# High and low rows of the activations as one 512-column product in the second layer's output and feed-forward projections

## The reference, cut to what matters

```python
def sq_relu_mlp(h, w1, w2):
    return jnp.square(jax.nn.relu(h @ w1)) @ w2
...
        xs = xs + g1 * ox
        xs = xs + g2 * sq_relu_mlp(rms_norm(xs, norm_mlp_g[l]) * (1 + sc2) + sh2, mlp_w1[l], mlp_w2[l])
```

## Time and profile before

| | us |
|---|---|
| median of 3 runs | 1467.81 |
| lowest and highest run | 1464.56, 1473.18 |
| profiled execution, its time | 1474.42 |
| profiled execution, its span | 1472.6 |
| TensorE busy in the span | 1405.8 (95%) |
| VectorE busy | 768.9 (52%) |
| ScalarE busy | 698.8 (47%) |

### The profile page before, as it was taken

How to read it: one execution, slowest core, us unless ns; L and a number is a source line. 1 busy time by engine, 2 the same in 40 slices (tenths; PEclk the granted TensorE clock), 3 DMA queues, 4 the chain that set the end, 5 groups by cost and what they waited for, 6 DMA issues and landing times.

```text
span 1472.6 us, 22615 instructions
## 1 busy us (share of the span) xinstructions
PE 1405.8 (95%) x8302; PEld 1144.3 (78%) x8302; DVE 768.9 (52%) x1227; ACT 698.8 (47%) x1102; POOL 297.5 (20%) x302
## 2 busy tenths in 40 slices
PE   6899999989899999999999999999998998999998
PEld 3677777757688888777868888888887766899997
DVE  4644889884355555453264423344326545665564
ACT  4358888867344444332254312233135544653543
POOL 2000124252455666450300000000120000200001
PEclk9999999999999999999999999999999999999999
DMA  9522232320653344532322332323233210465553
GB/s 333 160 72 74 84 88 84 86 60 27 230 170 116 116 144 129 183 134 86 108 72 87 98 95 91 100 86 100 88 99 105 95 58 1 144 185 179 180 185 102
DMA packets 138009, 170.59 MB, mean 116 GB/s; under 512 B 10912, under 2 KB 121760, under 8 KB 137920
## 3 DMA queue, kind: packets, MB, share of 16 engines
q1 hardware_dynamic: 137312, 169.18, 36.4%
q0 software_dynamic: 608, 0.19, 0.1%
HBM read 168.30 MB, written 1.05 MB: 115 GB/s over the span
## 4 chain that ended last, share of the span: by engine, by line
PE 74%; ACT 8%; DVE 8%; issue 4%; DMA 3%; POOL 1%; SPq 1%; ACTq 0%; DVEq 0%; POOLq 0%
PE bank L2000 53%; PE bank L2337 3%; PE bank L2325 3%; PE bank L1957 2%; ACT w_hi L827 2%; DMA raw<-in_w_mod 2%; DVE w_lo L1364 2%; DVE qkv L1388 1%; PE bank L2354 1%; PE bank L2186 1%; PE bank L2279 1%; PE bank L2201 1%; POOL qkv L679 1%; PE bank L2303 1%; ACT l_i L1057 1%
## 5 line engine op out<-in xcount | busy, mean ns | idle before, releaser
L1364 DVE TENSOR_TENSOR w_lo<-raw,w_hi 128x1024 fp32r<-128x1024 f32 x216 | 269.0, 1246 | 456.6 <-ACT w_hi L827 456.4
L827 ACT ACTIVATE w_hi<-raw 128x1024 fp32r<-128x1024 f32 x216 | 228.5, 1058 | 461.6 <-PE bank L2000 461.2
L2000 PE MATMUL bank<-h_hi,w_hi 128*128 128x512 f32 (+1 forms) x1024 | 379.5, 371 | 18.9 <-ACT h_hi L1026 8.0
L2000 PE MATMUL bank<-h_hi,w_lo 128*128 128x512 f32 (+1 forms) x1024 | 370.3, 362 | 0.0
L2000 PE MATMUL bank<-h_lo,w_hi 128*128 128x512 f32 (+1 forms) x1024 | 365.7, 364 | 2.8 <-DVE h_lo L1566 1.9
L2000 PEld LDWEIGHTS bank<-h_hi,w_hi 128*128 128x128 f32 x1024 | 195.7, 191 | 68.4 <-issue 29.0
L2000 PEld LDWEIGHTS bank<-h_lo,w_hi 128*128 128x128 f32 x1024 | 193.5, 191 | 38.1 <-DVE h_lo L1566 3.0
L2000 PEld LDWEIGHTS bank<-h_hi,w_lo 128*128 128x128 f32 x1024 | 195.4, 191 | 31.9
L647 POOL TENSOR_TENSOR n_sq<-xT 128x512 f32<-128x512 f32 (+1 forms) x24 | 23.3, 971 | 749.9 <-DVE xT L1425 748.9
L2000 PE MATMUL bank<-hid_hi,w_hi 128*128 128x512 f32 (+1 forms) x512 | 173.4, 339 | 1.0 <-DVE w_lo L1364 1.0
L2000 PE MATMUL bank<-hid_hi,w_lo 128*128 128x512 f32 (+1 forms) x512 | 172.8, 337 | 0.0
(11 more groups left out here) (306 smaller groups left out, 2100.7 us busy)
## 6 DMA issues: line engine op xcount, KB each, us to landing
raw<-in_mlp_w SPq DMA_DIRECT2D x128, 512.0 KB, 3.5
raw<-in_w_mod SPq DMA_DIRECT2D x80, 512.0 KB, 4.4
raw<-in_even_w_in SPq DMA_DIRECT2D x48, 512.0 KB, 3.6
first_w<-in_w_mod SPq DMA_DIRECT2D x16, 512.0 KB, 11.6
raw<-in_even_w_out SPq DMA_DIRECT2D x16, 512.0 KB, 3.4
raw<-in_attn_w_qkv SPq DMA_DIRECT2D x16, 512.0 KB, 3.4
raw<-in_attn_w_o SPq DMA_DIRECT2D x8, 512.0 KB, 3.4
xin<-in_ctx SPq DMA_DIRECT2D x2, 512.0 KB, 5.5
```

The source lines that it names most:

```text
L827: act.activation(w_hi[:, j % SPLIT], raw[:, j % RAW], ACT.Copy).then_inc(hi_ready, 1)
L1364: dve.tensor_tensor(w_lo[:, j % SPLIT], raw[:, j % RAW], w_hi[:, j % SPLIT].bitcast(F32), ALU.subtract).then_inc(split_done, 1)
L2000: return pe.matmul(bank[2 * pair + t][:, 0:T - n0], w[:, slot, k, t * P:(t + 1) * P], x_[:, n0:T], start=(kk == 0 and first), stop=(kk == ...
```

## The change

In `wo`, `up10`, `up11`, `down10` and `down11` (`joined`), the high and low rows of an activation tile, which now lie in one buffer (`h_both`, `hid_both`, `att_both`, at the old addresses), are streamed as one moving operand of 2 x 256 columns over `w_hi`: one matmul of 512 columns on one weight load in place of two of 256 on two loads. `w_hi*x_hi` falls into columns 0 to 255 of the bank and `w_hi*x_lo` into 256 to 511; `w_lo*x_hi` is added to the first half as before. The first pair of `up10` keeps three matmuls, its low pass going to the second half.

The halves are added when the bank is read. In `up`, ACT copies the second half to `relu`, DVE adds the first half to it, waits for its own write, and one `scalar_tensor_tensor` computes max(r, 0) * r. In `wo` and `down`, DVE runs its update of `xT` twice, once for each half, with a wait for its own write between.

```diff
+def joined(s):
+    return s["name"][:3] in ("up1", "wo") or s["name"][:5] == "down1"
...
-        hid_hi = F("hid_hi", 0, [16, T], F32R)
-        hid_lo = F("hid_lo", 32, [16, T], F32R)
+        hid_both = F("hid_both", 0, [2, 16, T], F32R)
+        hid_hi, hid_lo = hid_both[:, 0], hid_both[:, 1]
...
+        def two_rows(a_, b_):
+            return bass.AP(a_.tensor, a_.offset, [a_.ap[0], [b_.offset - a_.offset, 2], a_.ap[-1]])
...
+                        if joined(s):
+                            act.activation(relu[:, 2 * pair + t, n0:T], bank[2 * pair + t][:, T - n0:T], ACT.Copy).then_inc(s_relu, 1)
+                            continue
...
-                        dve.tensor_tensor(r_, r_, r_, ALU.mult).then_inc(s_sq, 1)
+                        if joined(s):
+                            dve.tensor_tensor(r_, bank[2 * pair + t][:, 0:T - n0], r_, ALU.add).then_inc(s_sum, 1)
+                            dve.wait_ge(s_sum, it * 4 + (s["up"] - SEG["up10"]["up"] + 2 * pair + t + 1))
+                            ins = dve.scalar_tensor_tensor(out=r_, in0=r_, scalar=0.0, in1=r_, op0=ALU.max, op1=ALU.mult)
+                        else:
+                            ins = dve.tensor_tensor(r_, r_, r_, ALU.mult)
+                        ins.then_inc(s_sq, 1)
...
-                            ins = dve.scalar_tensor_tensor(
-                                out=y, in0=bank[2 * pair + t][:, t0 - c0:t1 - c0],
-                                scalar=modv[:, layer, part, bass.ds(tl, 1), v:v + 1].rearrange("p a c -> p (a c)"), in1=y, op0=ALU.mult, op1=ALU.add)
+                            for p0 in (0, T - c0) if joined(s) else (0,):
+                                ins = dve.scalar_tensor_tensor(
+                                    out=y, in0=bank[2 * pair + t][:, p0 + t0 - c0:p0 + t1 - c0],
+                                    scalar=modv[:, layer, part, bass.ds(tl, 1), v:v + 1].rearrange("p a c -> p (a c)"), in1=y, op0=ALU.mult, op1=ALU.add)
+                                if joined(s) and not p0:
+                                    ins.then_inc(s_part, 1)
+                                    dve.wait_ge(s_part, it * 4 + (parts_before(s) + 2 * pair + t + 1))
...
+            def both_parts(s, j, k, t, hi, lo, n0):
+                pair, kk = j // s["upp"], j % s["upp"] * UNIT_K + k
+                hk, lk = (h[kk // 8][:, kk % 8] if isinstance(h, tuple) else h[:, kk] for h in (hi, lo))
+                x_ = two_rows(hk, lk)[:, :, n0:T]
+                return pe.matmul(bank[2 * pair + t][:, :].rearrange("p (a c) -> p a c", a=2), w_hi[:, j % SPLIT, k, t * P:(t + 1) * P],
+                                 x_, start=(kk == 0), stop=False)
...
             def tile_rows(s, j, k, t, hi, lo, n0):
+                if joined(s):
+                    both_parts(s, j, k, t, hi, lo, n0)
+                    return one_pass(s, j, k, t, w_lo, hi, n0, last=True)
                 one_pass(s, j, k, t, w_hi, hi, n0, first=True)
                 one_pass(s, j, k, t, w_hi, lo, n0)
                 return one_pass(s, j, k, t, w_lo, hi, n0, last=True)
...
-                        mm = one_pass(s, j, k, t, w_hi, lo, n0, last=True)
+                        mm = one_pass(s, j, k, t, w_hi, lo, n0, last=True, c0=T - n0 if joined(s) else 0)
```

More of the change, by code:

```diff
@@ L207, in build @@
         gy = F("gy", 80, [8, T])
-        h_hi = F("h_hi", 96, [KT, T], F32R)
-        h_lo = F("h_lo", 112, [KT, T], F32R)
+        h_both = F("h_both", 96, [2, KT, T], F32R)
+        h_hi, h_lo = h_both[:, 0], h_both[:, 1]
         assert free + 128 * KB <= nc.sbuf_usable_end
@@ L261, in build @@
         v1_tok = F("v1_tok", 24, [4, NT, P])
-        att_hi = F("att_hi", 32, [8, T], F32R)
-        att_lo = F("att_lo", 48, [8, T], F32R)
+        att_both = F("att_both", 32, [2, 8, T], F32R)
+        att_hi, att_lo = att_both[:, 0], att_both[:, 1]
         prob = F("prob", 72, [2, T])
@@ L293, in build @@
         s_wg = sem("s_wg")
+        s_part = sem("s_part")
+        s_sum = sem("s_sum")
         s_acc = sem("s_acc")
@@ L1424, in evac, with parts_before @@
                             y = dyn(xT, tl, t0, t1)
-                            ins = dve.scalar_tensor_tensor(
-                                out=y, in0=bank[2 * pair + t][:, t0 - c0:t1 - c0],
-                                scalar=modv[:, layer, part, bass.ds(tl, 1), v:v + 1].rearrange("p a c -> p (a c)"),
-                                in1=y, op0=ALU.mult, op1=ALU.add)
+                            for p0 in (0, T - c0) if joined(s) else (0,):
+                                ins = dve.scalar_tensor_tensor(
+                                    out=y, in0=bank[2 * pair + t][:, p0 + t0 - c0:p0 + t1 - c0],
+                                    scalar=modv[:, layer, part, bass.ds(tl, 1), v:v + 1].rearrange("p a c -> p (a c)"),
+                                    in1=y, op0=ALU.mult, op1=ALU.add)
+                                if joined(s) and not p0:
+                                    ins.then_inc(s_part, 1)
+                                    dve.wait_ge(s_part, it * 4 + (parts_before(s) + 2 * pair + t + 1))
                         ins.then_inc(evac_done, 1)
+            def parts_before(s):
+                return 8 * ("wo", "down10", "down11").index(s["name"])
             def segment(s, last=False, done=0):
@@ L1993, in unit, with one_pass @@
                 mm.then_inc(slot_free, 1)
-            def one_pass(s, j, k, t, w, h, n0, first=False, last=False, slot=None):
+            def one_pass(s, j, k, t, w, h, n0, first=False, last=False, slot=None, c0=0):
                 pair, kk = j // s["upp"], j % s["upp"] * UNIT_K + k
@@ L1999, in one_pass @@
                 x_ = h[kk // 8][:, kk % 8] if isinstance(h, tuple) else h[:, kk]
-                return pe.matmul(bank[2 * pair + t][:, 0:T - n0], w[:, slot, k, t * P:(t + 1) * P], x_[:, n0:T],
+                return pe.matmul(bank[2 * pair + t][:, c0:c0 + T - n0], w[:, slot, k, t * P:(t + 1) * P], x_[:, n0:T],
                                  start=(kk == 0 and first), stop=(kk == s["kt"] - 1 and last))
+            def both_parts(s, j, k, t, hi, lo, n0):
[4 more added lines that the diff above has]
+                                 x_, start=(kk == 0), stop=False)
             def tile_rows(s, j, k, t, hi, lo, n0):
+                if joined(s):
+                    both_parts(s, j, k, t, hi, lo, n0)
+                    return one_pass(s, j, k, t, w_lo, hi, n0, last=True)
                 one_pass(s, j, k, t, w_hi, hi, n0, first=True)
```

## The result

| | before | after |
|---|---|---|
| median of the runs side by side, us | 1466.71 (4 runs) | 1483.18 (4 runs) |
| lowest and highest | 1464.56, 1473.18 | 1479.70, 1485.33 |
| profiled execution, time and span | 1474.42, 1472.6 | 1479.70, 1477.9 |

The changed kernel is slower: ratio 1.0091, 95% interval 1.007 to 1.0112 (the two medians alone would give 1.0112). On 1467.8 us that is 1481.2 (1478.1 to 1484.3), against a forecast of 1480.2. The two spans differ by only 5.3, because the profiled execution of before was its slowest and that of after its fastest. What comes ahead of `wo`, which the change does not touch, took 1246.7 us in the one and 1240.6 in the other. So the segments from `wo` to the output, called layer 1 from here on, are compared one by one.

A forecast was written before the change was run, and what follows sets the result against it. TensorE, busy 95%, was taken to bound the kernel, with the evacuation on the way to the next weights in `up`. 0 + 8.1 + 3.3 + 1.0 = 12.4 us on 1467.8 gave 1480.2 us, range 1470 to 1489.

The forecast's parts named there:

- The formula of the loop: In `up`, stalls come at every other pair and two pairs take W + C, C being paid eight times.
- Term 2: Longer evacuation by DVE lengthens C in `up`: 8 x 1.02 = 8.1 us more (6.2 to 10.6).
- C: In `up`, time from a pair's end to the start of the pair after next, through weights and evacuation; 6.09 us before.
- Term 1: TensorE's stream, two matmuls joined in 560 tile steps: 0 us (-1.2 to +3.0).
- W: In `up`, the time of one pair's matmuls; 5.74 us before.
- Term 3: Evacuations between two `w_lo` in `down` and `wo`, longer updates stalling TensorE: +3.3 us (0.9 to 4.5).
- The low row of `rope`: DVE's wait for its own write: a dependent operation starts 0.03 us after the other's end, as in `rope`.
- Term 4: Ends of `wo` and `down11`, one more update and a wait of 0.51 us each: +1.0 us (0.8 to 1.3).
- The quick stream: Rival: the joined stream is much quicker, a step taking 320 ns, 33 less in `down`; 1471.6 us; chance 12%.
- That `up` does not feel the adds: Rival: C in `up` ends in something else, so term 2 goes; 1472 us; chance 7%.
- The clock: Rival: longer stalls in `up` lower TensorE's clock, some 1.7 us lost eight times, 14 in all; 1494 us; chance 5%.

The follow-up runs named there:

- the one trace of before: First profile of the unchanged kernel, layer 1 in 219.24 us; the other is the same kernel profiled once more, 217.66 us.
- `up` alone: The whole change in `up10` and `up11` only, other segments as in the kernel before: ratio 1.0079, layer 1 227.10 us; timed again 1.0062, 226.29 us.
- the addition alone: Against the kernel before: three separate 256-column matmuls kept, low rows' product in columns 256 to 511, halves added by the changed evacuation; ratio 1.0067, layer 1 229.80 us.
- whole change again: The changed kernel, no edit, timed again against the kernel before: ratio 1.0111, layer 1 231.06 us.
- the second batch: The change in `up10` and `up11` only, and in `wo`, `down10` and `down11` only, each against the kernel before: ratios 1.0079 and 1.0059.

## Why the prediction was right

The forecast of 1480.2 (+0.8%) was made by four terms. The main one held and its mechanism is shown; of the others two were too low and one far too high, and that the sum comes out so close is in part luck. The terms are measured below by the kernel with the joined matmul alone, which has the stream of the changed kernel and the evacuation of before.

**The formula of the loop held.** Two pairs took 12.8 us for the 12.9 forecast, and the stalls came at every other pair, eight in all, each released by `w_lo`. They are 1.1 to 1.6 us as gaps from start to start, and at most 1.3 by the view of waits, a little short of the 1.3 to 1.7 forecast.

**Term 2, C in `up`: 8 x 0.91 = 7.3 where 8.1 was forecast.** `up10` and `up11` are 7.5 us longer than with the joined matmul alone, of which 0.2 is the first pair of `up10`, so the eight C show in the time as well. The term was a little high because the max-square takes 0.425 us on average where L1425 had suggested 0.478, and a pair has two of them. From the groups of after (columns as in the earlier trace rows):

```profile
L1421 DVE SCALAR_TENSOR_TENSOR relu<-relu 128x256 f32<-128x256 f32 x32 | 13.6, 425 | 1.1
L1419 DVE TENSOR_TENSOR relu<-bank,relu 128x256 f32<-128x256 f32 x32 | 13.3, 417 | 0.0
L1594 DVE SCALAR_TENSOR_TENSOR h_both<-n_x,modv,h_both 128x256 fp32r<-128x256 f32 x40 | 17.7, 478 | 0.5 <-ACT h_both L1040 0.4
```

That the updates of `xT` read a bank is not the reason: L1594 reads none and takes 478 ns as well. Both L1594 and the updates read their scalar from `modv`, where the max-square has the constant 0.0; no run tests this difference by itself. The 0.03 for a wait on DVE's own write was right (1292.41 + 0.42 to 1292.87, and 1293.21 + 0.42 to 1293.66).

**Term 1, TensorE's stream: forecast 0, measured +1.4 to +3.0, in the upper half of its bounds by the one trace of before, at their end by the other.** The joined matmul alone shows it. My reason for 0 was that columns cost and loads do not, which held; what I mis-sized is the pace that is lost. I had put the quick pace of 340 ns a step as a share of before's steps and given it no weight, but the joined step has one pace only, 353 ns, and whatever ran quicker before is slowed to it. In `up` it counts in W, which was 5.76 in some pairs of before behind a stall and 5.95 in others, and is 5.94 in those of after.

**Term 3, evacuations in `wo` and `down`: forecast 3.3, measured 0.8, and not by its mechanism.** The step that failed is "in the loops the second update computes its addresses behind the wait, so I take 0.18": four updates take 1.91 in the loop of `down10`, as 1.89 with waits of 0.03 had it for the written-out body, and the stall of 0.3 that I had placed in `down10` is not there. In `wo`, where I had found no slack, the four pairs start as with the joined matmul alone (5.73, 5.65 and 5.69 apart in both). The low row of `rope` held for all of it. By the rule of the Trainium skill ("VectorE: DVE Perf Modes", section "The DRAIN you can't avoid") that I had weighed at this place, a wait between chained operations adds nothing: with 0.03 behind the end of the operation the trace nearly agrees, and the rule was the better guide than my 0.18. Counted from start to start, though, an update that waits for the one before takes 0.51 and one that does not 0.39, so against independent operations the wait is not free.

The 0.8 are three stalls of some 0.27, one in `wo` and two in `down11`, each behind a `w_lo` that took 1.42 to 1.71 us for 1.23. These `w_lo` start while POOL adds up squares for the norm, which it does behind the now longer evacuation. Before, POOL's work fell on other `w_lo`, which took 1.26 to 1.53. I had not thought of either.

**Term 4, the ends: forecast 1.0, measured 1.4.** At the output two updates stand in the chain for one, and the stretch is 5.12 for 4.61, +0.51, exactly half of the term. At the end of `wo` it is +0.91 from the last matmul to the norm's first. The chain that ended last there, in after and then with the joined matmul alone (columns as in the earlier trace rows):

```profile
1259.01 1.68 DVE w_lo L1378
...
1261.12 0.50 DVE xT L1446
...
1261.75 0.62 POOL n_sq L658
...
1265.78 0.70 PE bank L2103 x2
```
```profile
1258.23 1.23 DVE w_lo L1378
...
1259.99 0.61 POOL n_sq L658
...
1263.84 0.70 PE bank L2103 x2
```

From `w_lo` to TensorE it is 6.77 for 5.61. The second update is 0.53 of the difference, where 0.51 was forecast; the slower `w_lo` is 0.45, which holds the 0.27 of term 3 too, and POOL's own part, 4.03 for 3.85, is 0.18.

**What no term had: 0.4 from the clock.** In after the norm and the first pair of `up10` are 0.20 and 0.17 longer than with the joined matmul alone. The granted clock has a mean of 0.66 in this norm, TensorE having idled 1.93 us before it, where before has 1.00 and an idle time of 1.12.

By the traces the sum is thus 7.3 for C, 0.8 and 1.4 for terms 3 and 4, 0.4 for the clock, and 1.4 to 3.0 for the stream: 11.3 to 12.9, against 11.4 and 12.9 by the two traces of before and 12.4 of the forecast. Terms 2 and 3 were 0.8 and 2.5 too high; terms 1 and 4 and the clock were too low by 2.2 to 3.8 together and took it back.

**The rivals.** The quick stream would have shown under 335 ns a step, and a gain in the joined matmul alone; it showed 353 and +0.2%. That `up` does not feel the adds is refuted by `up` alone (+7.9 us) and by the addition alone. The clock does not fall by the stalls in `up`: it is granted at 1.00 through all of `up11`, and through `up10` behind its first pair. What the rival did not say is the norm. With TensorE's idle time of 1.9 to 2.0 us before it, the granted clock fell within the norm in three traces of six (after, whole change again, addition alone), for 0.4, 0.8 and 2.0 us; in the seven with 0.9 to 1.3 it did not. The weight loads that are busy all through `down10` spoke for the quick stream and meant nothing: with a third of them gone TensorE's pace is what it was.

**What stays open.** What sets the pace of separate 256-column matmuls, 113 or 118 ns, and why it changes within a segment, no run here tells. The difference between two profiles of the kernel before in layer 1 (1.6 us, nearly all in `down10`) comes from it, and it is why term 1 is known only as 1.4 to 3.0. That POOL slows the three `w_lo` is read from their overlap and tested by no run of its own. Why the medians of the second batch stood 4 to 6 us above their traces is open as well.

## What to carry to other kernels

Count the columns that go through TensorE, not the instructions: here 560 matmuls and 560 weight loads fewer were worth nothing, because the same 768 columns went through in each step. Work saved on one engine is paid on another, so look at what stands between a freed buffer and the next matmul: 0.92 us more on DVE, in a chain that ends last eight times, was most of the loss. That chain was there before the change, and putting the next weights ahead of the evacuation's last steps hid both the old stalls and the new ones; try the order of the queue before you change the arithmetic.

## What the runs showed of the hardware that I had not expected

- Separate float32r matmuls of 256 columns run at 340.0 or 353.8 ns for three, and one segment changed from one to the other between two steps, at a granted clock of 1.00. A step of 512 and 256 columns takes 353 ns in every trace.
- A stall costs TensorE some 0.1 us beyond its own length: behind it the second matmul starts 0.33 us after the first where it otherwise starts 0.23 after (512 columns), or 0.22 where it is otherwise 0.11 to 0.12 (256 columns), at a granted clock of 1.00.
- Where DVE and POOL overlap, at least one of them is slower. A `w_lo` that starts while POOL adds for the norm takes 1.71 us for 1.23, as in `down11` below, and 1.68 in `wo`; a POOL add that starts during a `w_lo` takes 1.79 for 0.73, and that `w_lo` keeps its 1.22. Rows of DVE's and of POOL's timeline:

```profile
1449.66 1.71 DVE L1378 TENSOR_TENSOR w_lo<-raw,w_hi 128x1024 fp32r<-128x1024 f32 x1 [1.47 <-ACT w_hi L838]
```
```profile
1449.56 0.73 POOL L660 TENSOR_TENSOR n_sq<-n_sq 128x256 f32<-128x256 f32 x1
```
